# First heads' chain two blocks forward, ScalarE's function sets loaded by hand, gate values normalised within the second heads, and weights rounded one block earlier

## The reference, cut to what matters

```python
# first block, per head: log-space decays of the recurrence
f = sigmoid(hf); g = lb + (1 - lb) * f; log_g = log(g); k = 1 - g
q = silu(hq) * 128 ** -0.5
o = hgrn2_scan(q, k, hi, log_g)
y_a = rms_norm(o, hg_norm_w) * silu(hg)
merged = gate_a * (y_a @ w_branch_a) + gate_b * (y_b @ w_branch_b)
# second block: the gate values
u, v = split(gelu(h @ w_in_uv))
v = (v - mean(v)) * rsqrt(var(v) + 1e-5) * ln_g + ln_b
y_a = u * (w_s @ v + b_s)
```

## Time and profile before

| | |
|---|---|
| median of 3 runs | 2975.06 us (2974.98 to 2975.60) |
| the profiled execution | 2977.24 us |
| its span | 2975.5 us |
| TensorE busy | 2881.9 us, 97% |
| VectorE, ScalarE busy | 2172.1 us (73%), 1505.1 us (51%) |
| GpSimd busy | 123.6 us (4%) |
| mean granted TensorE clock | 0.987 |
| HBM | 174 GB/s over the span |

### The profile page before, as it was taken

One profiled execution on the slowest core, in us unless ns is written; L12 is line 12 of the kernel. 1 busy time (PEld: TensorE's weight loads), 2 busy tenths in 40 slices (PEclk: granted clock), 3 DMA queues, 4 the chain that ended last, 5 costly groups with the idle time before them and its releaser, 6 DMA issues.

```text
span 2975.5 us, 42894 instructions
## 1 busy us (share of the span) xinstructions
PE 2881.9 (97%) x16334; PEld 2470.8 (83%) x16334; DVE 2172.1 (73%) x3307; ACT 1505.1 (51%) x2256; POOL 123.6 (4%) x121
## 2 busy tenths in 40 slices
PE   7999999999999999999998999999999999999997
PEld 6888888878888888888887888888888888888886
DVE  6777777778767777777786666667867887777775
ACT  5555554556554444444464454545555555555554
POOL 0000000000100000000040000000010000000001
PEclk9999999999999999999999999999999999999999
DMA  6444444445555555555564555565555565655553
GB/s 216 154 147 154 152 146 152 149 140 184 185 187 188 191 188 188 191 189 187 191 199 126 175 164 178 158 179 172 187 185 172 183 194 189 191 185 194 188 191 107
DMA packets 157020, 520.22 MB, mean 175 GB/s; under 512 B 28944, under 2 KB 31376, under 8 KB 156816
## 3 DMA queue, kind: packets, MB, share of 16 engines
q1 hardware_dynamic: 155376, 513.90, 53.7%
q10 hardware_dynamic: 1440, 3.59, 0.3%
HBM read 515.32 MB, written 2.10 MB: 174 GB/s over the span
## 4 chain that ended last, share of the span: by engine, by line
PE 68%; DVE 20%; ACT 7%; issue 4%; DMA 0%; SPq 0%; DVEq 0%; ACTq 0%; POOL 0%; POOLq 0%
PE acc L346 30%; PE acc L351 15%; DVE w_lo L1059 8%; PE psT L346 7%; PE psX L346 7%; ACT w_hi L676 4%; PE psT L351 3%; PE psX L351 3%; DVE work L1065 1%; DVE probs L1133 1%; DVE HS L1202 1%; ACT probs L726 1%; DVE soft L1134 1%; DVE work L1071 1%; DVE HS L1211 1%
## 5 line engine op out<-in xcount | busy, mean ns | idle before, releaser
L1059 DVE TENSOR_TENSOR w_lo<-w_raw,w_hi 128x1024 fp32r<-128x1024 f32 (+1 forms) x960 | 1173.9, 1226 | 602.3 <-ACT w_hi L676 590.6
L676 ACT ACTIVATE w_hi<-w_raw 128x1024 fp32r<-128x1024 f32 (+1 forms) x960 | 1005.2, 1053 | 738.6 <-PE acc L346 553.1
L346 PE MATMUL acc<-XU,w_hi 128*128 128x512 f32 x3472 | 1141.4, 401 | 3.9 <-issue 3.4
L351 PEld LDWEIGHTS acc<-XU,w_lo 128*128 128x128 f32 x3472 | 660.2, 190 | 153.1
L346 PE MATMUL acc<-XY,w_hi 128*128 128x512 f32 x2112 | 693.7, 401 | 11.9 <-DVE G L1065 4.6
L351 PE MATMUL acc<-XU,w_lo 128*128 128x256 f32 x3472 | 689.1, 280 | 0.0
L346 PEld LDWEIGHTS acc<-XU,w_hi 128*128 128x128 f32 x3472 | 550.5, 191 | 11.1 <-issue 7.3
L351 PEld LDWEIGHTS acc<-XY,w_lo 128*128 128x128 f32 x2112 | 399.9, 189 | 94.7 <-DVE XY L1251 3.4
L351 PE MATMUL acc<-XY,w_lo 128*128 128x256 f32 x2112 | 418.0, 279 | 3.1 <-DVE XY L1251 3.1
L346 PEld LDWEIGHTS acc<-XY,w_hi 128*128 128x128 f32 x2112 | 332.7, 190 | 23.6 <-issue 8.5
L346 PE MATMUL psT<-XY,w_hi 128*128 128x512 f32 x632 | 209.9, 397 | 5.7 <-DVE w_lo L1059 5.2
(11 more groups left out here) (233 smaller groups left out, 2555.4 us busy)
## 6 DMA issues: line engine op xcount, KB each, us to landing
w_raw<-in_weights SPq DMA_DIRECT2D x956, 512.0 KB, 3.5
bias<-in_rel_bias SPq DMA_DIRECT2D x8, 384.0 KB, 5.0
bias<-in_rpb_back SPq DMA_DIRECT2D x32, 96.0 KB, 6.2
w_raw<-in_weights SPq DMA_DIRECT2D x8, 384.0 KB, 3.1
hT<-in_x_t SPq DMA_DIRECT2D x8, 256.0 KB, 7.4
out_dram<-G ACTq DMA_DIRECT2D x4, 512.0 KB, 3.1
G<-in_range_sums ACTq DMA_DIRECT2D x1, 576.0 KB, 3.4
G<-in_pair_masks ACTq DMA_DIRECT2D x1, 576.0 KB, 4.5
```

Source lines behind the costliest of these rows:

```text
L346: return nc.tensor.matmul(bank[:, :], hi[:, k, col:col + P], X[:, k0 + k, :], start=first and k == 0, stop=last and k == nk - 1 and k % 2 ...
L351: return nc.tensor.matmul(bank[:, 0:T], lo[:, k, col:col + P], X[:, k0 + k, 0:T], start=False, stop=last and k == nk - 1 and k % 2 == 0, s ...
L676: act.activation(w_hi[s][:, 0:n], w_raw[s][:, 0:n], ACT.Copy).then_inc(hi_done, 1)
L1059: V.tensor_tensor(w_lo[s][:, 0:n], w_raw[s][:, 0:n], w_hi[s][:, 0:n].bitcast(F32), ALU.subtract).then_inc(lo_ready, 1)
```

## The change

It has four parts.

1. `heads1`. The stream brings the forget gate's tile first and the query's second (`starts` is `[1, 0, ...]`). The transposes of the log gates and the first decay product come after blocks 5 and 6 instead of 7 and 8, all pair products two blocks earlier and in step with VectorE's and GpSimd's parts, the tile product after 17, the scan's output after 18, its sum of squares after 20. VectorE masks pair product k in step 8 + 2k. The bias's memset moves to step 9. The norm's Ln, Exp and products move from step 21 to 20.
2. Function sets. ScalarE loads the sets with explicit instructions: per round of `heads1` sigmoid in step 0, Ln and sigmoid again in step 3, the set with Ln and Exp (`natural_log_exp_and_others`) in step 5; per round of `heads2` Gelu in step 0 and the Ln-and-Exp set in step 1; one load each at the entry of `branches`, after the output projections, before the last step of `ffn1last`, after the two norms, and around `ffn2`.
3. Gate values. The two norms move into step 1 of `gmv`, behind the first tile's sum. The value sums are issued between the blocks of `gmv` from block 5 on and after blocks 0 and 1 of `heads2`'s first round; centring stands in its steps 2 to 5 (two tiles each), the sums of squares after its blocks 4 and 6, the reciprocal deviation in ScalarE's step 6, the normalised value in VectorE's step 7. In that round the transposes, the mix product and what follows it come three to four blocks later. Squares use four buffers instead of two. The sixteen scalings of `hT` (1341) move from `gmv` to steps 10 and 12 of the second heads.
4. Rounding. ScalarE waits for the block five before the one it rounds, b-1, instead of for block b. The two cross buffers are now taken in turn over phase ends too.

```diff
     def round_block(p, i, b):
...
-                    act.wait_ge(w_used, p.block(i, b) + 1)
+                    act.wait_ge(w_used, p.block(i, c) - SLOTS + 1)
...
-                act.activation(cross[:, c % 2, :], bank[:, T:2 * T], ACT.Copy).then_inc(cross_ready, 1)
+                act.activation(cross[:, p.cross(i, c) % 2, :], bank[:, T:2 * T], ACT.Copy).then_inc(cross_ready, 1)
```

```diff
             after1 = {
-                7: [transpose_pair(wk(0), "lg_ready", "lgT_full")],
-                8: [decays(0)],
+                5: [transpose_pair(wk(0), "lg_ready", "lgT_full")],
+                6: [decays(0)],
+                8: [pair_products(0), decays(1)],
                 9: [transpose_pair(wk(5), "vi_ready", "vT_full")],
-                10: [pair_products(0), decays(1)],
-                12: [pair_products(1), decays(2)],
+                10: [pair_products(1), decays(2)],
+                12: [pair_products(2), decays(3)],
                 13: [scores(0, P, 1)],
-                14: [pair_products(2), decays(3), transpose_pair(wk(5), "avz_ready", "avT_full", "v_ready")],
+                14: [pair_products(3), transpose_pair(wk(5), "avz_ready", "avT_full", "v_ready")],
                 15: [scores(1, T, 1)],
-                16: [pair_products(3)],
-                18: [tile_pairs],
-                19: [scan_out, prob_transposes(0, 1)],
-                20: [attend(0, 1), prob_transposes(1, 1)],
-                21: [scan_rms, attend(1, 1)],
+                17: [tile_pairs],
+                18: [scan_out],
+                19: [prob_transposes(0, 1)],
+                20: [scan_rms, attend(0, 1), prob_transposes(1, 1)],
+                21: [attend(1, 1)],
             }
```

```diff
 # ScalarE, heads1
+                    if i and b == 0:
+                        act.preload_act_table(ACT.Sigmoid)
                     if b == (1 if i else 4):
-                        sigmoid_of(2, "hq_z", "hq_sig", i)
+                        sigmoid_of(0, "hf_z", "hf_sig", i)
                     if b == (3 if i else 4):
-                        act.wait_ge(S("q_ready"), i + 1)
-                        sigmoid_of(0, "hf_z", "hf_sig", i)
+                        act.wait_ge(S("g_ready"), i + 1)
+                        sigmoid_of(2, "hq_z", "hq_sig", i)
+                        act.preload_act_table(ACT.Ln)
+                        act.activation(wk(0), wk(0), ACT.Ln).then_inc(S("lg_ready"), 1)
+                        act.preload_act_table(ACT.Sigmoid)
                     if b == 5:
-                        act.wait_ge(S("g_ready"), i + 1)
-                        sigmoid_of(3, "hg_z", "hg_sig", i)
-                        act.activation(wk(0), wk(0), ACT.Ln).then_inc(S("lg_ready"), 1)
-                    if b == 7:
                         act.wait_ge(S("lgT_full"), i + 1)
                         act.activation(lg_hi[:, :, :], psT[:, 0:T], ACT.Copy).then_inc(S("lg_hi_ready"), 1)
+                        act.wait_ge(S("q_ready"), i + 1)
+                        sigmoid_of(3, "hg_z", "hg_sig", i)
+                        act.preload_act_table_set(LOG_EXP)
```

```diff
 # TensorE, gmv and the first round of heads2
+                if b % 2 and b >= 5:
+                    value_sum((b - 5) // 2)
...
+            first2 = after2 | {
+                0: [value_sums(value_sum, 6)],
+                1: [value_sums(value_sum, 7)],
+                4: [value_sums(value_square_sum, 0, 1, 2, 3)],
+                6: [value_sums(value_square_sum, 4, 5, 6, 7)],
+                7: [scores(0, T, 2), transpose_pair(wk(3), "vh_ready", "vh_full")],
+                8: [mix, transpose_pair(wk(5), "avz_ready2", "avT_full2")],
+            }
 # VectorE, gmv
                 if b % 2:
+                    tile_sum(p, 0, t, b, t, acc[t % 2], value)
+                    if b == 1:
+                        two_norms()
+                    mark(V.tensor_tensor(value, value, rs[:, :], ALU.mult), S("gv_z"), t + 1)
 # VectorE, heads2
+                    if i == 0 and 2 <= b < 6:
+                        center(2 * b - 4)
+                        center(2 * b - 3)
+                    if b in (10, 12):
+                        j = 2 * i + (b - 10) // 2
+                        link(V.scalar_tensor_tensor(hT[:, j, :], hT[:, j, :], cols[:, C_FIN1 + j:C_FIN1 + j + 1], rs1[:, :],
+                                                    ALU.mult, ALU.mult))
```

More of the change, by code:

```diff
@@ L591, in _, with value_sum, value_square_sum @@
             ffn("ffn1last", 0, XY, XU, S("act1_ready"))
+            def value_sum(t):
+                pe.wait_ge(S("gv_ready"), t + 1)
+                done = nc.tensor.matmul(psT[:, 0:T], ones[:, :], G[:, 24 + t, :], start=t == 0, stop=t == HEADS - 1)
+                if t == HEADS - 1:
+                    done.then_inc(S("gv_sum"), 1)
+            def value_square_sum(t):
+                pe.wait_ge(S("gv_sq"), t + 1)
+                nc.tensor.matmul(psE[:, 0:T], ones[:, :], value_squares[t % 4], start=t == 0, stop=t == HEADS - 1)\
+                  .then_inc(S("gv_sq_used"), 1)
             p = ph["gmv"]
@@ L604, in _ @@
                     rms_sum(1, psX)
[L605 to L613, removed]
+                if b % 2 and b >= 5:
+                    value_sum((b - 5) // 2)
             def mix(i):
+                if i == 0:
+                    pe.wait_ge(S("ws_in"), 16)
                 pe.wait_ge(S("vn_ready"), i + 1)
@@ L621, in mix, with value_sums, job @@
                 done.then_inc(S("mix_full"), 1)
+            def value_sums(which, *tiles):
+                def job(i):
+                    for t in tiles:
+                        which(t)
+                return job
             after2 = {
@@ L868, in _, with two_norms @@
             ffn1("ffn1last", 0)
+            act.preload_act_table_set(LOG_EXP)
             next_operand(ph["ffn1last"], KD - 1)
[L872 to L877 removed]
+            def two_norms():
+                act.wait_ge(stat_done, 3)
+                link(act.activation(rs[:, :], psS[:, 0:T], ACT.Ln, bias=eps_rms, scale=1.0 / D))
+                act.activation(rs1[:, :], rs[:, :], ACT.Exp, scale=-0.5).then_inc(S("rs1_ready"), 1)
+                act.wait_ge(S("ms2_ready"), 1)
+                link(act.activation(rs[:, :], wk(8), ACT.Ln, bias=eps_rms, scale=1.0 / D))
+                act.activation(rs[:, :], rs[:, :], ACT.Exp, scale=-0.5).then_inc(rs_ready, 1)
+                act.preload_act_table(ACT.Gelu_apprx_tanh)
             p = ph["gmv"]
@@ L899, in _ @@
                         act.activation(wk(0), wk(0), ACT.Gelu_apprx_tanh).then_inc(S("u_ready"), 1)
-                    if b == 4:
+                        act.preload_act_table_set(LOG_EXP)
+                    if i == 0 and b == 6:
+                        act.wait_ge(S("gv_sq_used"), HEADS)
+                        rstd(rsv, psE[:, 0:T], WIDTH, eps_ln, wk(4), S("gv_rstd"))
+                    if b == (4 if i else 7):
                         act.wait_ge(S("vh_full"), i + 1)
                         act.activation(v_nat[:, :, :], psT[:, 0:T], ACT.Copy).then_inc(S("vn_ready"), 1)
-                    if b == 6:
+                    if b == (6 if i else 9):
                         act.wait_ge(S("ya_z2"), i + 1)
@@ L1064, in tile_sum @@
                 dve.wait_ge(cross_ready, p.cross(i, c) + 1 - RAW // 2)
-                mark(V.tensor_tensor(dst, bank[:, 0:T], cross[:, c % 2, :], ALU.add), acc_free,
+                mark(V.tensor_tensor(dst, bank[:, 0:T], cross[:, p.cross(i, c) % 2, :], ALU.add), acc_free,
                      p.tile(i, t) + 1 + TILE_CREDIT)
@@ L1220, in _ @@
                                 link(ins)
+                    if b == 9:
+                        scaled_tile(p, i, 4, b, 4, bank, wk(7), S("k_z"), i + 1)
+                        dve.wait_ge(S("bias1_in"), 16 * i + 16)
+                        link(V.memset(bias[0:64, :, P:P + 64], MASKED))
                     if b == 11:
@@ L1227, in _ @@
                         softmax_back(0, P, 1, i)
[L1228 to L1234 removed]
+                    if b in (15, 17, 19, 21):
                         n = (b - 15) // 2
@@ L1352, in _, with center @@
-            dve.wait_ge(S("gv_rstd"), 1)
-            dve.wait_ge(S("bs_in"), 32)
+                    value = G[:, 24 + t, :]
+                    tile_sum(p, 0, t, b, t, acc[t % 2], value)
+                    if b == 1:
+                        two_norms()
+                    mark(V.tensor_tensor(value, value, rs[:, :], ALU.mult), S("gv_z"), t + 1)
+            def center(t):
+                value = G[:, 24 + t, :]
+                link(V.tensor_tensor(value, value, wk(8), ALU.subtract))
+                if t >= 4:
+                    dve.wait_ge(S("gv_sq_used"), t - 3)
+                mark(V.tensor_tensor(value_squares[t % 4], value, value, ALU.mult), S("gv_sq"), t + 1)
@@ L1479, in weight_block @@
         t = b // 2
-        starts = [0, 1, 3, 2, 5, 4, 6]
+        starts = [1, 0, 3, 2, 5, 4, 6]
```

168 lines of the change are left out of this document (85 added, 83 removed).

## The result

| | before | changed |
|---|---|---|
| median of 6 runs | 2975.02 us (2974.15 to 2977.39) | 2924.43 us (2921.83 to 2924.89) |
| profiled execution, its span | 2977.24, 2975.5 us | 2924.89, 2923.1 us |
| mean granted clock | 0.987 | 0.993 |

The ratio is 0.9827, with a 95% interval of 0.9815 to 0.984. The forecast of 2926.5 us is 2 us off. And the experiments show that the sum booked the largest saving to the wrong part of the change.

What follows compares the result with a forecast made beforehand. TensorE, busy 2881.9 of 2975.5 us, was taken as the bound, leaving its waits and half-clock time to win. Savings of 12 + 5.0 + 5.0 + 7.6 + 5.7 + 6.1 + 6.0 + 1.3 = 48.7 gave 2926.5 us, range 2899 to 2952.

Steps and rivals of the forecast that it cites:

- The size of the waits in the new first heads: First heads: TensorE waits 1.7 us before the decay product and about 1.7 before the scan output, each round.
- Such a gap at full clock stays at full clock: First heads: waits of 1.7 us leave TensorE at 2.4 GHz, so a round loses 3.5 us instead of 5.4.
- rival A: First heads: both waits exceed 2.5 us and half clock follows each, 25 us more, 2951 us; chance 0.16.
- First heads: -12 us: First heads: reordering saves 1.9 us in each of seven rounds, 13, less a costlier first round.
- The entry of the branches: Entry of the first branches: the 3.10 us wait and slow work behind it disappear with the earlier norm, -5.0 us.
- Rival E: Sets are ignored and loads stay where they stood: 2939 us; chance 0.05.
- Rival D: First heads: loads come on top of the automatic ones, half clock follows: 2979 us, slower; chance 0.05.
- The rounding's other three places: Earlier rounding saves 5.0 us at the value phase's entry, 7.6 in the second heads, 5.7 in the last phase.
- Rival C: Earlier rounding brings nothing because ScalarE's own queue holds it up: 18.3 us fall away, 2945 us; chance 0.08.
- The value phase: Value phase: first tile's sum ahead of the norms saves 6.1 us; value sums laid between blocks save 6.0.
- Rival B: First heads: both waits vanish, by less contention with GpSimd or less waiting on ScalarE: 2899 us; chance 0.18.
- the first exponentials, which stay: First heads, VectorE's stretch from decay product to second softmax front: 2.0 us of its 5.0 idle, taken as remaining.

Runs made afterwards that it cites:

- automatic loads: Changed kernel with every function set loaded taken out except the very first: 2919.9 us, ratio 0.9812.
- the sets by hand with the norm in its old step: Changed kernel with the first heads as before and two sets a round loaded there: 2893.9 us, ratio 0.9727.
- part 4 alone: Kernel before the change, with only the earlier rounding and the cross buffers taken in turn over phase ends: 2916.3 us, ratio 0.9801.
- the old first heads: Changed kernel with order and steps of the first heads as before and no sets there: 2901.0 us, ratio 0.9749.
- the old rounding wait: Changed kernel in which ScalarE again rounds block b+4 only when block b is done: 2980.7 us, ratio 1.0018.

## Why the prediction came out right, and what in it was wrong

**The size of the waits in the new first heads.** The chain to the decay product was laid out right: 1.7 forecast, 1.61 measured. So was the chain to the scan, 1.7 forecast, 2.05 measured, with exactly the operations named (front, exponentials, two roundings, cross copy, copy).

**"Such a gap at full clock stays at full clock" failed.** The rows had 1.04 and 2.2 on one side and 2.8 on the other, and I put 1.7 with the first. The gap came out at 2.05, and half clock followed it in seven of eight rounds, 1.5 us each and 10.5 in all: half of rival A. The stretch still won 12.4 us of the 17, by two things that the forecast did not have: two rounds of the kernel before took 80.3 us and not the 79.07 of the one that was read, and the first round became 1.5 us shorter where 0.9 more of loss was forecast.

**"First heads: -12 us", as the worth of the reordering, failed, and it is the step that matters.** The losses of the new order were worked out with the earlier rounding already in them, those of the old order were read from a trace without it, and the difference was booked to part 1. The section on the rounding then said of each late sum that up to 2.3 us could be won, and listed three places; the first heads, with two late sums a round, were not in the list. Part 4 by itself is worth 36 us there; with part 4 in place, part 1 and its sets cost 23.4 (2924.4 against 2901.0). The total could come out right because the combination had been worked out and not its parts, and it came within 2 us because the misses of the stretches cancel.

**The function sets.** In the prediction the loads in the first heads were part of the chain and not priced against what ScalarE does without them. They cost 9.9 us there. The entry of the branches was forecast at -5.0 and came out at -5.2 (the two blocks before 668.84 took 10.89 us with their waits, the same two after 5.69), and by two runs either half of the change would have done: the norm's move with automatic loads (5.69), or the sets by hand with the norm in its old step (5.80). The end, -1.3, and some 3 us between the value phase's norm sum and the second branches are the sets'. Rival E is out: the loads stand where they were placed, and with automatic loads the kernel gets faster, not slower. Rival D is out too: no load stands next to one placed by hand.

**The rounding's other three places** were right. The entry of the value phase: -5.0 forecast, -6.0 in the run of part 4 alone. The second heads: the 5.6 are gone in that run, and so are 1.5 of the 2.0; the other 0.5 lie behind the second branches and stay. The last phase: 5.7 forecast, 8.3 measured between the second branches and the last sum. The waits of the earlier trace rows explain 5.7, a fifth wait of 0.87 before the transposes that the prediction did not count (it was for ScalarE) and smaller ones 1.2; 1.4 show in no wait. Rival C is out by 59 us.

**The value phase**: -6.1 and -6.0 forecast. Between the run of part 4 alone and that with the old first heads 12.0 were measured, but 2.9 of them are the sets' (-23.9 against -21.0), so that some 9 are left for part 3: the term was a quarter too large, and that 12.1 and 12.0 agree is luck. In the run with the old rounding wait the same stretch shows only -3.7. With the rounding late, the interleaved sums and the transposes behind them wait for VectorE (1.7 and 2.7 us in its list of waits), and in the second heads a sum waits 0.7 us in every round where it waited 0.2 before. So without part 4 less than a third of the 12.0 is left.

**Rival B** (no waits in the first heads, 2899) had the right instinct and the wrong reason: the chain was indeed without slack, but not for VectorE's work alone. Its "less contention with GpSimd" named something real: 0.9 us for each long product. But the changed kernel has as many of them as the one before, 24; they became fewer only where the old order met the earlier rounding. The prediction had the order of ScalarE's queue in its sum twice, as 2.0 us for "the first exponentials, which stay" and as two roundings ahead of the copy, and did not ask whether they have to be there. Moving the exponentials behind the rounding removed both.

## What to carry to other kernels

Price each part of a change against the kernel that already has the other parts: a wait that two parts can both cure may not be credited to the one that the diff puts in the foreground. Where an engine that is behind waits for another that also waits, look at the second one's queue: work that depends on nothing belongs ahead of work that waits for the late engine (here the rounding ahead of the exponentials, 15 us). Moving a product behind one more block helps only if that product alone is late; when a whole engine is, the next reader of it meets the same delay. Where two engines start on the same signal, look whether one of them takes longer when it starts second: an engine that is behind then falls back further.

## What the runs showed of the hardware

**The clock.** Single gaps of TensorE in the rounds of the first heads left the clock at 2.4 GHz wherever they were up to 1.61 us long (1.55 and 1.61 most often), in every kernel here. Behind 2.81 us, in the kernel before, it fell to 1.2 GHz eight times of eight. In between it went both ways: 1.82 was followed by 1.2 GHz in the first round of two kernels and not in two others, 2.05 seven times of eight in the changed kernel and five of eight with automatic loads, 3.3 six times of seven with the old rounding wait, 2.09 at the entry of the first branches in two kernels and not in a third. So the length of the gap alone does not decide, and what else does is not shown. Two gaps of 0.98 and 1.05 with one group of transposes between them were followed by 1.2 GHz in three of six rounds; 0.64 and 1.05 with a block between them never. Filling 1.4 us of the 2.05 with products that nobody reads made the kernel 10.1 us faster.

**VectorE beside GpSimd.** The product of decays and query, 128x512, took VectorE 0.69 us, and 1.47 to 1.59 when it started while GpSimd's product on the same tile was running: so in all 416 of thirteen kernels.
